# HGRN2: the order of GpSimd's products, of ScalarE's exponents and of the fourth tile's split

## The reference

```python
log_f = logaddexp(log(lb), log1p(-lb) + log_sigmoid(f))
k = (1 - lb) * sigmoid(-f)
G = cumsum(log_f) within a chunk
q_dec, k_dec = q * exp(G), k * exp(G_last - G)
attn[l, s] = sum_d q[l, d] * exp(G[l, d] - G[s, d]) * k[s, d]      # s <= l
o = q_dec @ state + attn @ v
state = exp(G_last) * state + k_dec^T @ v
y = head_rms_norm(o) * silu(gate);  out = y @ w_out
```

## Time and profile before

| | us |
|---|---|
| median of 3 runs | 1978.09 (1976.34 to 1978.68) |
| the profiled execution | 1975.95 |
| its span, first to last instruction | 1973.9 |
| HGRN2 phase, first take of f to last y | 834.1 to 1137.4 |
| one of the middle heads | 37.6 |

### The profile page before, as it was taken

How to read it: one execution, slowest core, us unless ns; L and a number is a source line. 1 busy time by engine, 2 the same in 40 slices (tenths; PEclk the granted TensorE clock), 3 DMA queues, 4 the chain that set the end, 5 groups by cost and what they waited for, 6 DMA issues and landing times. The chain is left out here.

```text
span 1973.9 us, 24375 instructions
## 1 busy us (share of the span) xinstructions
PE 1805.9 (91%) x8342; PEld 1423.5 (72%) x8342; DVE 1106.6 (56%) x1719; ACT 830.5 (42%) x1400; POOL 401.3 (20%) x325
## 2 busy tenths in 40 slices
PE   7997998889999899898998698999989899998988
PEld 5666887667888688677777576888868666666755
DVE  6535444277666433867777537666633576785434
ACT  5544545354333322554454335433322442443342
POOL 0332453101111000035335400111100011221100
PEclk9998999999999899999999799999989998999979
DMA  5111100322233222211110031223232321011002
GB/s 195 51 46 54 43 12 22 110 82 87 97 99 99 76 97 96 76 53 53 53 64 32 0 126 66 88 98 99 65 107 96 107 67 41 23 65 64 22 33 74
DMA packets 39776, 140.06 MB, mean 71 GB/s; under 512 B 4384, under 2 KB 4640, under 8 KB 39584
## 3 DMA queue, kind: packets, MB, share of 16 engines
q1 hardware_dynamic: 39712, 139.23, 21.1%
HBM read 137.11 MB, written 2.10 MB: 71 GB/s over the span
## 5 line engine op out<-in xcount | busy, mean ns | idle before, releaser
L187 PE MATMUL bank<-u_high,w_high 128*128 128x512 f32 x1448 | 602.7, 416 | 47.3 <-DVE u_low L239 18.0
L189 PE MATMUL bank<-u_high,w_low 128*128 128x512 f32 x1448 | 574.4, 397 | 0.0
L188 PE MATMUL bank<-u_low,w_high 128*128 128x512 f32 x1448 | 574.2, 397 | 0.0
L160 DVE TENSOR_TENSOR w_low<-w_ring,w_high 128x1024 fp32r<-128x1024 f32 x186 | 238.2, 1286 | 267.1 <-ACT w_high L151 264.1
L187 PEld LDWEIGHTS bank<-u_high,w_high 128*128 128x128 f32 x1448 | 278.3, 192 | 135.1 <-issue 51.3
L151 ACT ACTIVATE w_high<-w_ring 128x1024 fp32r<-128x1024 f32 x249 | 259.8, 1052 | 274.2 <-PE bank L189 258.6
L189 PEld LDWEIGHTS bank<-u_high,w_low 128*128 128x128 f32 x1448 | 277.6, 192 | 60.9
L188 PEld LDWEIGHTS bank<-u_low,w_high 128*128 128x128 f32 x1448 | 279.1, 193 | 54.7 <-issue 3.8
L160 POOL TENSOR_TENSOR w_low<-w_ring,w_high 128x1024 fp32r<-128x1024 f32 x63 | 149.9, 2387 | 643.3 <-ACT w_high L151 643.3
L706 ACT ACTIVATE conv_up<-bank,col_sb 128x512 f32<-128x512 f32 x88 | 68.5, 779 | 271.6 <-DVE bank L724 271.6
L187 PE MATMUL bank<-src_high_down,w_high 128*128 128x512 f32 x352 | 139.5, 396 | 16.4 <-DVE src_low_down L469 16.4
(11 more groups left out here) (415 smaller groups left out, 2501.4 us busy)
## 6 DMA issues: line engine op xcount, KB each, us to landing
w_ring<-ffn_up SPq DMA_DIRECT2D x88, 512.0 KB, 3.6
w_ring<-ffn_down SPq DMA_DIRECT2D x44, 512.0 KB, 3.7
w_ring<-c_in SPq DMA_DIRECT2D x32, 512.0 KB, 3.7
w_ring<-g_in SPq DMA_DIRECT2D x16, 512.0 KB, 4.1
w_ring<-m_in SPq DMA_DIRECT2D x12, 512.0 KB, 5.2
w_ring<-fox_in SPq DMA_DIRECT2D x12, 512.0 KB, 3.8
w_ring<-dsa_in SPq DMA_DIRECT2D x12, 512.0 KB, 3.8
w_ring<-ab_out SPq DMA_DIRECT2D x8, 512.0 KB, 3.7
```

Of the source, the lines that this page charges most:

```text
L160: eng.tensor_tensor(low[:, :], self.w[:, s, :], high[:, :].bitcast(F32), ALU.subtract).then_inc(self.w_split, 1)
L187: nc.tensor.matmul(out, a[0], b[0], start=start, stop=False)
L188: nc.tensor.matmul(out, a[0], b[1], start=False, stop=False)
L189: return nc.tensor.matmul(out, a[1], b[0], start=False, stop=stop)
```

## The change

In DVE's program the kdf subtraction moves behind the four diffs, and `low(h+1, 3)` moves from behind them into slot 3, ahead of the take of q. In ACT's program E and the exponent of kdf move behind the exponents of level 3, and `high(h+1, 3)` from behind level 0's to the same place, ahead of them. In GpSimd's program kd and qd move behind the products of level 6; kd signals `kd_ready` by itself, and qd a new semaphore `qd_ready`. PE waits for the head's first diff instead of `g_ready` in front of the k by q product, and for `qd_ready` too ahead of the first state product. No instruction of computation is added or removed.

```diff
 # PE
                 pe.wait_ge(sig_ready, h + 1)
-                pe.wait_ge(g_ready, h + 1)
+                pe.wait_ge(diff_ready, NL * h + 1)
...
                             pe.wait_ge(s_ready, h + 1)
+                            pe.wait_ge(qd_ready, h + 1)
 # ScalarE
-                act.wait_ge(g_ready, h + 1)
-                nc.scalar.activation(E[:, :], G[:, :], ACT.Exp)
-                nc.scalar.activation(kdf[:, :], kdf[:, :], ACT.Exp, scale=-1.0).then_inc(e_ready, 1)
                 for l, b in enumerate(LEVELS):
...
-                    if nxt and l == 0:
-                        high(h + 1, 3)
+                    if l == 3:
+                        if nxt:
+                            high(h + 1, 3)
+                        act.wait_ge(g_ready, h + 1)
+                        nc.scalar.activation(E[:, :], G[:, :], ACT.Exp)
+                        nc.scalar.activation(kdf[:, :], kdf[:, :], ACT.Exp, scale=-1.0).then_inc(e_ready, 1)
 # GpSimd
-                pool.wait_ge(e_ready, h + 1)
-                nc.gpsimd.tensor_tensor(kd[:, :], kk[:, :], kdf[:, :], ALU.mult)
-                nc.gpsimd.tensor_tensor(qd[:, :], q[:, :], E[:, :], ALU.mult).then_inc(kd_ready, 1)
                 for l, b in enumerate(LEVELS):
...
+                pool.wait_ge(e_ready, h + 1)
+                nc.gpsimd.tensor_tensor(kd[:, :], kk[:, :], kdf[:, :], ALU.mult).then_inc(kd_ready, 1)
+                nc.gpsimd.tensor_tensor(qd[:, :], q[:, :], E[:, :], ALU.mult).then_inc(qd_ready, 1)
 # VectorE
-                nc.vector.tensor_tensor(chunks(kdf), chunks(G), chunks(G)[:, :, P - 1:P].to_broadcast([P, NT, P]), ALU.subtract).then_inc(g_ready, 1)
                 for l in range(R):
                     diff(h, l)
-                if nxt:
-                    low(h + 1, 3)
-
+                nc.vector.tensor_tensor(chunks(kdf), chunks(G), chunks(G)[:, :, P - 1:P].to_broadcast([P, NT, P]), ALU.subtract).then_inc(g_ready, 1)
...
                     elif nxt and l == 3:
+                        low(h + 1, 3)
                         take(h + 1, 1, qraw, q_taken)
```

More of the change, by code:

```diff
@@ L791, in hgrn2 @@
     f_taken, q_taken, g_taken, raw_ready, v_turned = (sem(f"c_{s}") for s in ("f_taken", "q_taken", "g_taken", "raw_ready", "v_turned"))
-    (f_clamped, act_prep, sig_ready, ft_ready, logf_ready, g_ready, e_ready, kd_ready, tr_done, kdt_ready, kv_done,
+    (f_clamped, act_prep, sig_ready, ft_ready, logf_ready, g_ready, e_ready, kd_ready, qd_ready, tr_done, kdt_ready, kv_done,
      s_ready, diff_ready, lexp_ready, x_ready, lv_done, at_done, o_done, osb_ready, osq_ready, nrm_done, rs_ready, y_ready,
      ch_act, ch_dve) = (sem("c_" + s) for s in (
-         "f_clamped act_prep sig_ready ft_ready logf_ready g_ready e_ready kd_ready tr_done kdt_ready kv_done "
+         "f_clamped act_prep sig_ready ft_ready logf_ready g_ready e_ready kd_ready qd_ready tr_done kdt_ready kv_done "
          "s_ready diff_ready lexp_ready x_ready lv_done at_done o_done osb_ready osq_ready nrm_done rs_ready y_ready "
```

## The result

The changed kernel takes 1963.88 us (median of 4 runs, 1959.56 to 1965.14) beside 1977.21 for the kernel before (4 runs): a ratio of 0.9929, 95% interval 0.9914 to 0.9945. That is some 14 us (11 to 17) faster. Forecast were 8.5 us, 1969.6, with a range from 1964 to 1976: the direction is right, but the gain was put too low, and the median lies just under the range.

What follows compares the result with a forecast made beforehand. PE sets the pace, with a 2.65 us hole before level 0. Gains of 6 x 0.7 (heads 0 to 5) + 0.4 + 1.6 + 2.3 = 8.5 us give a median of 1969.6 us; range 1964 to 1976.

Steps and rivals of the forecast that it cites:

- What bounds the kernel: HGRN2 heads: PE sets the pace; its largest hole, 2.65 us before level 0, waits for GpSimd's kd and qd.
- How DVE and GpSimd disturb each other: Shared SBUF access: DVE instructions with two SBUF inputs and GpSimd's run one after the other, in order of issue.
- The front: Up to level 0: with kd and qd gone, level 0 starts at 964.04 without waiting, 2.65 us early.
- Levels 0 to 4: DVE reacts 1.29 us after a level starts, PE needs 1.69 a level; the lead stays 2.7 to 2.9 us.
- Slots 3 and 4: DVE's lows before levels 5 and 6: lead falls to 1.65, then 0.73 us, with kd ahead of slot 4's low.
- rival "low first": Slot 4: DVE's low gets ahead of kd, six heads gain 1.3 us instead of 0.7; 1966 us, chance 0.27.
- The tail: After level 6: kd and qd are ready before PE needs them, all as before, leaving 0.7 us a head.
- third rival: DVE blocked by whole GpSimd instructions in slots 3, 4 and at the clamp, 0.4 to 1.0 us each; 1975 us, 0.17.
- Head 0's spell at half clock: Half-clock spell at head 0's level 0: expected gone, worth between 0 and 1.7 us, taken as 0.4.
- Head 6: No low in slot 4, so kd blocks nothing there; level 6 starts 1.6 us early.
- Head 7: Last head, without projections or lows: gains 2.3 us.
- The clock rival: PE's two waits, before levels 5 and 6, bring half-clock spells in heads 1 to 6; slower, 1990 us, chance 0.06.

Runs made afterwards that it cites:

- kernel with one memset: Changed kernel plus a tiny DVE memset, with a wait for it, in front of dif 4 (slot 0); 1967.9 us, 0.9952 of the kernel before.
- two memsets: Changed kernel plus two linked tiny DVE memsets in front of dif 4 (slot 0); 1970.88 us in one run.
- kernel with tile 0's low alone moved: Changed kernel with low(h+2, 0) moved out of slot 4, behind the gate's product, low(h+1, 3) staying in slot 3; 1950.72 us in one run.

## Why the prediction missed, point by point

- **What bounds the kernel**: right. PE sets the pace, and the hole in front of level 0 was 2.65 us; it is gone in every head that has projections (heads 0 to 6).
- **How DVE and GpSimd disturb each other**: right, and all runs bear it out: 2.26 for kd behind a low, 2.12 for a low behind kd, 1.27 for a dif behind a product. What it left out is the clamp (see the tail).
- **The front**: right to the hundredth, 2.95 us from the k by q product to level 0.
- **Levels 0 to 4: this is the step that failed.** It said that DVE reacts 1.29 us after a level starts and that a level with its piece of projection takes 1.69. Both came from levels for which PE had stood still; such a level's eight rows last 1.16 us, those of a level that follows without a break 1.06, with DVE's reaction at 1.19 and the next level after 1.59 (962.21 to 963.80). Head 0 of the trace before had that pace too, 1.58 from one level to the next:

```profile
859.59 1.05 PE L837 MATMUL bank<-c_X 128*128 128x128 f32 x8
...
861.17 1.05 PE L837 MATMUL bank<-c_X 128*128 128x128 f32 x8
```

  The 0.10 us were small as a term of the sum, and were not carried into the range. But they decided an order: dif 4 came 0.10 us ahead of the second product of level 2, and not a little behind it. In the prediction's own times the product was ahead by 0.06 (X 2 ready at 966.0, less 0.73, against dif 4 at 965.33), a margin that it did not name. That put DVE 0.6 us earlier in slot 0 already. The delay of 0.13 us that undoes it costs the whole 0.9 us by which a middle head was forecast too low.
- **Slots 3 and 4**: slot 3 right (1.24 us of wait, forecast 1.3, counted alike); slot 4 with the order the other way round and so 0.76 instead of 1.3. In head 0 it is as forecast, kd ahead and a low of 2.13. The kernel with one memset has both as forecast, 1.25 and 1.29.
- **The rival "low first"** is what happened in heads 1 to 5, at the upper end of its 1.3 to 1.6 us a head. Its 1966 took 1.3, and it was given 0.27. The argument against it was that kd and the low both follow from the end of slot 3's low, so that their order is given. It overlooked that the order at slot 3 itself can differ: with DVE earlier, it is the last product of level 5 (969.03, 1.70) that stands behind that low, and the two products of level 6 have still to come before kd.
- **The tail**: 0.3 us short. From level 6 to the first state product it was 4.85 and is 5.13. The clamp (974.75) ran into qd, which ends at 975.55, and took 1.09 instead of 0.43; the last two copies came later with it, so PE waits 0.22 for the states. In heads 1 to 5 of the kernel with one memset the clamp takes 0.43, and the tail 4.85. This was a part of the third rival, at a smaller price, and its sign, a clamp over 1 us, was there although the head gained more than forecast.
- **Head 0's spell at half clock**: gone, as expected (1.00 over the head). **Head 6**: forecast 1.6, measured 2.1, for the order again: with two memsets, which turn it round, it gains 1.5. **Head 7**: 2.3, right.
- **The clock rival**: the granted clock is 1.00 over heads 1 to 5 in spite of the two new waits, so this case was not met. The mechanism exists in this loop all the same: with GpSimd's part undone, and a wait of 4.09 us, the spell comes in every head. As a sign "clock under 1.00 in heads 1 to 6" was too wide: the stretch of head 6, from its k by q product to the last head's, stood at 0.88 in the kernel before and at 0.90 in the changed one.
- **The range** was too narrow: the low-first case with 1.6 us a head gives 13 to 14 us in all, or 1964, and that was made its very end.

What stays open: the spread between runs in the phases ahead of HGRN2 (over 9 us in the start of the phase, in unchanged code), which blurs all totals, has no cause here. Nor has the 0.10 us by which head 6's dif 4 comes earlier than the others'.

## What to carry to other kernels

When two engines take turns at a shared access, a schedule worked out from a trace has steps in it: look for the places where the two ask within about 0.1 us of each other, work out both orders to the end, and give both full weight. Take reaction times from rows in which the engine had not been waiting, if it will not wait in the changed kernel. And move one thing at a time: here GpSimd's order alone gives a shorter head than the whole change, because the split that was moved with it landed on the chain that then set the end.

## What was not expected of the hardware

That 0.13 us of delay on one instruction of DVE costs 0.9 us in each of five heads, 0.20 us no more than that, and 0.13 nothing in the two heads where it doesn't change the order. And that a `tensor_scalar` with one SBUF input and no second tensor (the clamp, 0.43 us alone) was held up by a GpSimd multiplication, which the prediction had in a rival only: 1.09 us with qd ahead of it, and 1.43 in the kernel with tile 0's low alone moved, where it is issued 0.13 us after qd:

```profile
962.54 1.43 DVE L1008 TENSOR_SCALAR c_f<-c_f 128x512 f32<-128x512 f32 x1
```

```profile
962.41 1.28 POOL L977 TENSOR_TENSOR c_qd<-c_q,c_E 128x512 f32<-128x512 f32 x1
```

The Trainium skill's page SBUF — State Buffer, section "Who interferes with whom", lists `tensor_scalar` among the operations that can enter a mode with two ports and then contend with GpSimd. These two rows agree.
